# Conditioning products of layer 1 and block 2: from TensorE to VectorE row scalars in a two-block transformer kernel

## The reference, cut to what matters

```python
cond = silu(c) @ w_ada[l] + b_ada[l]            # first block, l = 0, 1: 1024 -> 3072
shift, scale, gate_raw = split(cond, 3)
h = x * (1 + scale) + shift
proj = h @ w_in[l]
...
mod   = silu(c_2)     @ w_ada_2 + b_ada_2       # second block: 1024 -> 6144
mod_c = silu(c_ctx_2) @ w_ada_2 + b_ada_2       # the same matrix, a second vector
```

## Time and profile before

| | |
|---|---|
| median of 3 runs | 5348.12 us (5343.71 to 5350.91) |
| profiled execution | 5341.84 us, span of its trace 5340.1 us |
| mean granted TensorE clock | 0.884 of full speed |
| stage ada | 0 to 62 us |
| proj0, making of h | 62 to 87 us |
| proj0, 33 steps | 87 to 608 us |
| engines over the span | TensorE 84% busy, VectorE 30%, ScalarE 21%, GpSimd 14% |

### The profile page before, as it was taken

One profiled execution on the slowest core, in us unless ns is written; L12 is line 12 of the kernel. 1 busy time (PEld: TensorE's weight loads), 2 busy tenths in 40 slices (PEclk: granted clock), 3 DMA queues, 4 the chain that ended last, 5 costly groups with the idle time before them and its releaser, 6 DMA issues. The chain is left out here.

```text
span 5340.1 us, 76356 instructions
## 1 busy us (share of the span) xinstructions
PE 4483.6 (84%) x29176; PEld 2919.5 (55%) x29176; DVE 1614.9 (30%) x2633; ACT 1135.4 (21%) x1627; POOL 748.3 (14%) x523
## 2 busy tenths in 40 slices
PE   6999757879997997577799967777986999999972
PEld 3666646666665886466566635554452444444431
DVE  1000355442412005555414123443040111111117
ACT  1000243321212112333212132221011111111110
POOL 1111000102222220001022200000022010101014
PEclk8999879889998998788799976667977999999985
DMA  4334212412221222100022100001014999999977
GB/s 170 150 145 162 100 34 98 156 69 98 75 79 63 94 90 78 47 26 26 25 80 83 67 30 8 4 0 42 24 59 149 358 363 355 363 356 362 356 260 253
DMA packets 170078, 715.23 MB, mean 134 GB/s; under 512 B 26881, under 2 KB 28674, under 8 KB 134018
## 3 DMA queue, kind: packets, MB, share of 16 engines
q1 hardware_dynamic: 119714, 536.83, 27.7%
q10 hardware_dynamic: 25632, 93.33, 4.3%
q0 software_dynamic: 24512, 81.84, 4.2%
HBM read 584.95 MB, written 126.98 MB: 133 GB/s over the span
## 5 line engine op out<-in xcount | busy, mean ns | idle before, releaser
L400 PE MATMUL ps<-s_proj_hS,s_proj_wS 128*128 128x512 f32 x3216 | 761.7, 398 | 62.1 <-POOL s_proj_wS L312 62.1
L400 PEld LDWEIGHTS ps<-s_proj_hS,s_proj_wS 128*128 128x128 f32 x3216 | 605.1, 189 | 223.4 <-ACT s_proj_wS L361 63.0
L1806 PE MATMUL ps<-s_mix_hS,s_mix_wS 128*128 128x512 f32 x1536 | 394.5, 412 | 40.6 <-POOL s_mix_wS L1665 35.5
L1806 PEld LDWEIGHTS ps<-s_mix_hS,s_mix_wS 128*128 128x128 f32 x1536 | 291.1, 190 | 135.9 <-issue 48.8
L2668 PE MATMUL ps<-s_exp_gu,keep_hT 128*128 128x512 f32 x736 | 338.9, 603 | 16.2 <-DMA s_exp_gu<-in_w_gu_dram 14.7
L2652 PE MATMUL ps<-s_exp_wd,s_exp_aT 128*128 128x512 f32 x736 | 331.2, 593 | 1.9 <-ACT s_exp_aT L2578 1.9
L2673 PE MATMUL ps<-s_exp_gu,keep_hT 128*128 128x512 f32 x736 | 330.8, 592 | 0.0
L1665 POOL TENSOR_TENSOR s_mix_wS<-s_mix_w,s_mix_wS 128x1024 fp32r<-128x1024 f32 x96 | 230.6, 2403 | 584.7 <-ACT s_mix_wS L1674 584.7
L340 DVE COPY s_proj_o<-ps 128x512 f32<-128x512 f32 x66 | 45.6, 691 | 706.8 <-PE ps L400 706.8
L312 POOL TENSOR_TENSOR s_proj_wS<-s_proj_w,s_proj_wS 128x1024 fp32r<-128x1024 f32 x67 | 162.6, 2430 | 689.7 <-ACT s_proj_wS L361 689.7
L2618 DVE TENSOR_TENSOR s_exp_sg<-s_exp_sg,ps 128x256 f32<-128x256 f32 x92 | 38.8, 421 | 659.9 <-ACT s_exp_sg L2599 659.9
(11 more groups left out here) (440 smaller groups left out, 6427.2 us busy)
## 6 DMA issues: line engine op xcount, KB each, us to landing
s_exp_gu<-in_w_gu_dram SPq DMA_DIRECT2D x184, 1024.0 KB
s_exp_wd<-in_w_down_dram SPq DMA_DIRECT2D x92, 1024.0 KB
yrow<-keep_hT ACTq DMA_DIRECT2D x92, 512.0 KB, 9.4
s_proj_wa<-in_w_ada_dram SPq DMA_DIRECT2D x72, 512.0 KB, 4.6
s_proj_w<-in_w_in_dram SPq DMA_DIRECT2D x66, 512.0 KB
proj<-s_proj_o ACTq DMA_DIRECT2D x66, 512.0 KB
yrow<-keep_xT SPq DMA_DIRECT2D x4, 8192.0 KB
s_mix_w<-in_w_in_dram SPq DMA_DIRECT2D x64, 512.0 KB
```

The lines of the kernel that those rows point to most:

```text
L400: mm = pe.matmul(k.ps[:, 6 + half if last else 2 * b + half, :], wS[:, b, x, t, :], hS[:, y, t, half * HALF:(half + 1) * HALF], start=(t = ...
L1806: mm = pe.matmul(k.ps[:, bank, :], wS[:, b, u, x, :], src[:, v, x, :], start=(x == 0 and u + v == 0), stop=(x == KT - 1 and u == 1))
```

## The change

- Stage ada computes only layer 0's shift and scale: 16 slabs in 4 groups in place of 24 in 6. Layer 0's gate (slabs 16 to 23) moves into proj0.
- In proj0 TensorE no longer multiplies conditioning slabs. The 80 slabs form 10 groups of 8, one per round i = 0 to 9: four groups `ONE` (slabs 16 to 47, one vector, c) and six groups `TWO` (slabs 48 to 95, the two vectors of block 2).
- SP loads for a group 8 tiles, one per row tile c: of 8 slabs the 128 x 128 piece c each, 512 KB as 1024 pieces of 512 bytes. They go through a ring of 4 slots in `k.mix`; the load of tile c waits until tile c - 4 is used. Tiles 0 to 3 belong to step b = 0, tiles 4 to 7 to b = 1, and SP issues the tiles of a step after the weight load of the step two later. SP's list is fully unrolled.
- VectorE, after its copy of the step, forms acc = acc + tile * scalar for each of the 4 tiles and each vector: one scalar_tensor_tensor of 128 x 1024 each, the scalar being `k.silu`'s entry of the partition (tile 0: a tensor_scalar with no addition). This makes 4 per step in ONE and 8 per step in TWO, in two of three steps.
- TensorE, ahead of the main matmuls of the next round's b = 0 step, sums acc over the partitions: for each vector 8 matmuls with a 128 x 128 piece of acc as weights and a single column of ones as moving data. It first waits for the last accumulation of the round. VectorE copies the 8 or 16 columns into `k.cond`.
- Each vector is multiplied only with the matrix that it belongs to; before, all 3 were multiplied with every slab.

The diff, cut to its core:

```diff
 def modulation(k):
-    NG = NADA1 // GRP
+    NS = 2 * KT
+    NG = NS // GRP
 ...
 def projection(k, l):
-    R1, R2 = 1, 9
-    NX = (2 * NADA1 + NADA2 - NADA1) // (NB * (R2 - R1))
+    ONE, TWO = (2 * KT, 4), (2 * NADA1, 6)
+    NWA = 4
 ...
-            wa = s.sb("wa", [P, NX, KT, P])
-            row = s.sb("row", [3, NX * P])
+            acc, wa = k.mix[:, 0:2], k.mix[:, 2:2 + NWA]
 ...
+            parts = [(0, 1, ONE, None), (1, 2, ONE, ONE), (2, na, ONE, ONE), (na, na + 1, TWO, ONE), (na + 1, nb, TWO, TWO), (nb, NR, None, TWO)] if not l else \
 ...
+        def group(g, kind):
+            return (g - ONE[1], 2, TWO[0], range(1, 3)) if kind is TWO else (g, 1, ONE[0], range(0, 1))
 ...
         def _(sp):
+            def tiles(i, b, cur):
+                g, nv, s0, vs = group(i, cur)
+                for c in range(4 * b, 4 * b + 4):
+                    wait(sp, acc_ready[0], i * KT + (c - NWA + 1))
+                    if nv == 2:
+                        wait(sp, acc_ready[1], g * KT + (c - NWA + 1))
+                    sp.dma_start(wa[:, c % NWA].rearrange("p (g n) -> p g n", g=KT),
+                                 I["w_ada"][bass.ds(g * KT + s0, KT), :, c, :].rearrange("g p n -> p g n")).then_inc(ld_a[c % NWA], 16)
 ...
                 sp.dma_start(w[:, b], src).then_inc(ld_w[b], 16)
-                if ada:
-                    m = n - R1 * NB
-                    wait(sp, ada_ready, m)
-                    for x in range(NX):
-                        sp.dma_start(wa[:, x], I["w_ada"][m * NX + (NADA1 + x)]).then_inc(ld_a[x], 16)
+                late.append((i, b, cur))
+                if len(late) > 2 and late[-3][2]:
+                    tiles(*late[-3])
 ...
         def _(dve):
+                if old:
+                    g, nv, s0, vs = group(i - 1, old)
+                    wait(dve, ada_ready, i)
+                    dve.tensor_copy(k.cond[:, bass.ds(g * KT + s0, KT), vs[0]:vs[0] + nv],
+                                    k.ps[:, 7, 0:KT * nv].rearrange("p (v g) -> p g v", v=nv)).then_inc(ada_taken, 1)
+                if cur:
+                    g, nv, s0, vs = group(i, cur)
+                    for c in range(4 * b, 4 * b + 4):
+                        wait(dve, ld_a[c % NWA], i * 2 * 16 + (c // NWA + 1) * 16, 16)
+                        for v in range(nv):
+                            done, at = acc_ready[v], (g if v else i) * KT + c
+                            scale = k.silu[:, c, vs[v]:vs[v] + 1]
+                            if c:
+                                wait(dve, done, at)
+                                dve.scalar_tensor_tensor(acc[:, v], wa[:, c % NWA], scale, acc[:, v], ALU.mult, ALU.add).then_inc(done, 1)
+                            else:
+                                wait(dve, ada_ready, i)
+                                dve.tensor_scalar(acc[:, v], wa[:, 0], scale, None, ALU.mult).then_inc(done, 1)
 ...
         def _(pe):
+                if old:
+                    g, nv, s0, vs = group(i - 1, old)
+                    wait(pe, acc_ready[0], i * KT)
+                    if nv == 2:
+                        wait(pe, acc_ready[1], g * KT + KT)
+                    wait(pe, ada_taken, i - 1)
+                    for v in range(nv):
+                        for x in range(KT):
+                            mm = pe.matmul(k.ps[:, 7, v * KT + x:v * KT + x + 1], acc[:, v, x * P:(x + 1) * P], k.ones[:, 0:1],
+                                           start=True, stop=True)
+                    mm.then_inc(ada_ready, 1)
                 wait(pe, hi_ready, n + 1)
 ...
-                    for t in range(KT):
-                        mm = pe.matmul(k.ps[0:3, 6, 0:NX * P], k.silu[:, t, :], wa[:, :, t, :], start=(t == 0), stop=(t == KT - 1))
```

More of the change, by code:

```diff
@@ L1 @@
+import itertools
 from contextlib import ExitStack
@@ L213, in _ @@
             dve.wait_ge(ld_c, 32 + 16 * KT)
-            dve.tensor_tensor(k.cond[:, 0:NADA1], k.cond[:, 0:NADA1], k.bias[:, 0:NADA1].unsqueeze(2).to_broadcast([P, NADA1, 3]),
+            dve.tensor_tensor(k.cond[:, 0:NS], k.cond[:, 0:NS], k.bias[:, 0:NS].unsqueeze(2).to_broadcast([P, NS, 3]),
                               ALU.add).then_inc(own, 1)
@@ L269, in projection, with steps @@
         else:
-            wa = s.sb("wa", [P, NX, KT, P])
-            row = s.sb("row", [3, NX * P])
-            ld_a, ada_ready, ada_taken = [s.sem(f"ld_a{x}") for x in range(NX)], s.sem("ada_ready"), s.sem("ada_taken")
-            row_ready, turned = s.sem("row_ready"), s.sem("turned")
+            acc, wa = k.mix[:, 0:2], k.mix[:, 2:2 + NWA]
+            ld_a = [s.sem(f"ld_a{x}") for x in range(NWA)]
+            acc_ready, ada_ready, ada_taken = [s.sem("acc_ready0"), s.sem("acc_ready1")], s.sem("ada_ready"), s.sem("ada_taken")
         block = s.block()
-        def steps(eng):
+        def steps(eng, unrolled=False):
             NR = NSCAN // NB
[L279 to L284, removed]
+            na, nb = ONE[1], ONE[1] + TWO[1]
+            parts = [(0, 1, ONE, None), (1, 2, ONE, ONE), (2, na, ONE, ONE), (na, na + 1, TWO, ONE), (na + 1, nb, TWO, TWO), (nb, NR, None, TWO)] if not l else \
+                [(0, 1, None, None), (1, NR - 1, None, None), (NR - 1, NR, None, None)]
+            for a, z, cur, old in parts:
+                if z == a + 1 or (unrolled and not l):
+                    for i, b in itertools.product(range(a, z), range(NB)):
+                        yield i, b, cur if b < 2 else None, old if b == 0 else None
                 else:
@@ L287, in steps @@
                         for b in range(NB):
-                            yield i, b, ada
+                            yield i, b, cur if b < 2 else None, old if b == 0 else None
             if l:
-                yield NSCAN // NB, 0, False
+                yield NSCAN // NB, 0, None, None
+        def group(g, kind):
+            return (g - ONE[1], 2, TWO[0], range(1, 3)) if kind is TWO else (g, 1, ONE[0], range(0, 1))
         @block.sync
         def _(sp):
-            for i, b, ada in steps(sp):
+            def tiles(i, b, cur):
[6 more added lines that the diff above has]
+                                 I["w_ada"][bass.ds(g * KT + s0, KT), :, c, :].rearrange("g p n -> p g n")).then_inc(ld_a[c % NWA], 16)
+            late = []
+            for i, b, cur, old in steps(sp, unrolled=True):
                 n = i * NB + b
@@ L309, in _ @@
                 pool.tensor_tensor(hS[:, 1, t], o[:, t % NB], hS[:, 0, t], ALU.subtract).then_inc(hlo_p, 1)
-            for i, b, ada in steps(pool):
+            for i, b, cur, old in steps(pool):
                 wait(pool, hi_ready, i * NB + (b + 1))
@@ L332, in _ @@
             low(KT - 1)
-            for i, b, ada in steps(dve):
+            for i, b, cur, old in steps(dve):
                 n = i * NB + b
@@ L340, in _ @@
                 dve.tensor_copy(o[:, b, HALF:T], k.ps[:, 2 * b + 1, :]).then_inc(taken_v, 1)
[L341 to L348, removed]
@@ L349, in _ @@
-            if not l:
[L350 to L353, removed]
+                if old:
[3 more added lines that the diff above has]
+                                    k.ps[:, 7, 0:KT * nv].rearrange("p (v g) -> p g v", v=nv)).then_inc(ada_taken, 1)
@@ L355, in _ @@
+            if not l:
+                dve.wait_ge(ada_taken, ONE[1] + TWO[1])
+                for (s0, ng), v0, nv in ((ONE, 0, 1), (TWO, 1, 2)):
+                    at = k.cond[:, s0:s0 + ng * KT, v0:v0 + nv]
+                    dve.tensor_tensor(at, at, k.bias[:, s0:s0 + ng * KT].unsqueeze(2).to_broadcast([P, ng * KT, nv]),
+                                      ALU.add).then_inc(ada_taken, 1)
         @block.scalar
@@ L367, in _ @@
             high(0, 1)
-            for i, b, ada in steps(act):
+            for i, b, cur, old in steps(act):
                 n = i * NB + b
@@ L384, in _ @@
         def _(pe):
-            for i, b, ada in steps(pe):
+            for i, b, cur, old in steps(pe):
                 n = i * NB + b
                 last = isinstance(n, int) and n == NSCAN
+                if old:
[9 more added lines that the diff above has]
+                    mm.then_inc(ada_ready, 1)
                 wait(pe, hi_ready, n + 1)
@@ L403, in _ @@
                     mm.then_inc(half_ready, 1)
[L404 to L413, removed]
-                    for t in range(KT):
-                        mm = pe.matmul(k.ps[0:3, 6, 0:NX * P], k.silu[:, t, :], wa[:, :, t, :], start=(t == 0), stop=(t == KT - 1))
-                    mm.then_inc(ada_ready, 1)
 def chunks(ap):
```

## The result

The changed kernel takes 5214.94 us, the median of 4 runs (5208.75 to 5221.99), against 5349.51 us for the kernel before (4 runs, three of them the ones that the prediction started from). The ratio is 0.9743, with a 95% interval of 0.9718 to 0.9769: 2.6% faster. Of the cases named, rival A, no stall, 5219 us, is the nearest.

What follows compares the result with a forecast made beforehand. TensorE's own list was taken to bound the 33 steps; -149.0 - 15.9 + 35.5 + 18 + 15 = -96.4 us from 5341.84 gives 5245.4, forecast 5252 us on the median scale. Range 5214 to 5292 us.

Steps and rivals of the forecast that it cites:

- rival A: Two-vector rounds: GpSimd costs VectorE little, additions at 1.21 us, no stall; -129.4 us, 5219 us, chance 0.19.
- What bounds the kernel: In proj0's 33 steps TensorE is busy 520.83 of 521 us, so its own list is the time.
- the product removed: In proj0 conditioning product and turns leave TensorE's list, 149.0 us gained, all on the path.
- the first stage: Stage ada ends two groups earlier, 15.9 us gained.
- one-vector rounds: In ONE a VectorE step takes 8.4 us, under 11.2; sums ready at 19.6 of 22.4, cost 0.
- the DMA: Conditioning tiles as 512-byte pieces take 2.2 us each; the engines carry 26 of some 40 us a round, cost 0.
- SP's and ScalarE's lateness: In TWO SP's weight load goes out late and ScalarE waits some 4 us for it, cost 0.
- the bias additions: The two bias additions at the end lie beside the last store, cost 0.
- Step 4: VectorE's additions in TWO take 25.3 us against 22.4; TensorE stands 3.0 us before the sums of six rounds, 18 us.
- step 6: Queues: SP's held weight load, late copies and tile loads in proj0 are all covered, cost 0.
- Step 5: TensorE's clock falls after each of the six gaps before sums, 2.5 us each, 15 us added.
- Step 3: Row sums on TensorE, 256 records at 0.127 us plus 0.3 for each of 10 changes, 35.5 us added.

Runs made afterwards that it cites:

- Experiment 6: SP issues conditioning tiles after the weight load of the step three later, not two, against the changed kernel; 33 steps 435.1 us instead of 413.9.
- experiment 3: One-vector rounds of the changed kernel do their row-sum products twice, 32 records in place of 16; 33 steps 430.0 us instead of 413.9.
- experiments 4 and 7: Against the changed kernel: 4 returns layer 0's gate to stage ada, last copy 499.84, not 485.42; 7 loads 4 KB tile rows, 33 steps 410.9 us, not 413.9.
- experiment 5: VectorE adds a step's four tiles for the first vector, then the second, in place of alternating, against the changed kernel; 33 steps 466.4 us instead of 413.9.

## Why the prediction was wrong

**Right.** What bounds the kernel (TensorE's list, and nothing over it), the product removed (149.0 forecast, 149.3 measured) and the first stage (15.9 and 15.5). Covered work was covered: one-vector rounds, the DMA, SP's and ScalarE's lateness, the bias additions.

**Step 4, the step that failed.** The forecast let VectorE take 25.3 us for two steps against 22.4, and TensorE stand 3.0 us before six sums, 18 us. TensorE never stood. VectorE takes 21.6 us (384.13 to 405.70), and has 21.9 until the first weight load of the sums (406.01). Of the 3.7 us by which the forecast was over, additions 1.20 us apart, the lower bound, and not 1.28, make 1.1 over 14 of them; two tensor_scalars at 0.66, not 0.81, make 0.3; and the largest part, 2.1, is a low part that was charged and holds nothing up. The rest is in the copies. The forecast charged both low parts because it read in the earlier trace rows that the engines take turns, instruction by instruction. That holds for the low part of b = 0, and not for the one of b = 1, which comes at the seventh of eight additions. Its own step 6 had that slab late, and step 4 didn't use it; yet by the times given there, 4.6 us to land and 1.1 for the high part, the low part would have come some 5 us into the additions (an estimate), still among them. It took the real lateness, 7.6 us, and an order of turns that no row of before showed. Experiment 6 brings the low part forward and the stall appears, 1.5 us.

**Step 5, right in size and wrong in cause.** 15 us were forecast from the clock and 14.0 measured, but the forecast tied them to the idle time; had it dropped the stall, as rival A did, it would have dropped the clock's cost with it, and rival A's 5219 does. The clock falls with the block of 32 one-column records alone, without any idle time. Rival A plus that cost would have been 5234; the sums being 6 us cheaper and some 15 us gained behind the changed stages bring the measured time below both.

**Step 3, a size.** A record costs 0.109 us in a block of 32 at full clock (248.20 to 251.69) and 0.106 in one of 16 (106.71 to 108.41), where 0.127 was taken. The nearest row, the turns of 3 rows, came out too high; that each group of 6 held its own start and end is the likely reason. The Trainium skill (TensorE: Matmul & The Clock Gate, LDWEIGHTS) gives 107 ns for 128 columns; these runs agree with it, to 2 ns.

**The range.** The changed stages alone, 122.5 us, would have given 5225.6, inside the range and 26 us under the forecast. The time fell below its lower end, 5214, because of the 15 us behind them, for which the sum had no term and no run shows the reason. The lower end stood 5 us under rival A; room for cheaper sums, or 10 us for the stages behind, would either alone have held the result.

## What to carry to other kernels

- When work moves to an engine with room, add up that engine's list for the period in which its result is due, with the instructions of the engine that holds its own up, each placed at the time at which its own inputs arrive; charging every neighbour once a step was 2 us too much in 22.
- Products with 128 x 128 weights and one moving column cost 0.106 to 0.111 us a record here, in a block or between wide products. But a block of 32 brought TensorE's clock down for the wide products behind it in most cases, and two blocks of 16 with 5.7 us of wide work between them didn't in any. For the whole kernel the difference is not shown.
- An arrangement with 0.3 us of slack a round works until an unrelated load comes earlier: experiment 6 made a load earlier and lost 21 us.

## What the runs showed of the hardware that was not expected

- The granted clock fell from 2.4 to 1.2 GHz while TensorE was busy without a gap, 2.4 to 4.8 us after the first of 32 one-column float32 records: in 6 of 6 such blocks in the kernel after and in both its repeats, in 9 of 10 in experiment 3, in 5 of 6 in experiments 4 and 7, in none of the blocks of 16. The stretches last 3.4 or 6.8 us, and a step with one takes 1.5 or 3.2 us more than one without (16.4 or 18.0 against 14.85).
- VectorE and GpSimd take turns, but not always. A low part that arrives at the second or third operation of VectorE's run in a step gets its turn behind the running one and holds the next for 2.1 us, in all runs here. One that arrives at the sixth or seventh of eight waits until VectorE's run ends, 1.2 to 2.7 us (the 4.30 at 403.63 above), and VectorE loses nothing. With additions that wait for each other (experiment 5) it gets its turn at the fifth and sixth too. What decides between the two was not tried.
